# Another order of the work inside a turn of the chunked RWKV-7 scan, with the state update split into a part from keys and a part from betas

## The chip, the cores and the metric

The kernel runs on one core of a Trainium2 chip and computes two whole model blocks. The metric is the device time of one execution in microseconds (us). The change touches only one stage, the RWKV-7 scan of the first block.

## What is computed

The scan carries a 64x64 state S for each of 16 heads over the tokens, once forwards and once backwards (256 context tokens first, then 512 latent ones):

```python
def step(s, inp):
    r_t, w_t, kk_t, a_t, k_t, v_t = inp
    s_kk = jnp.einsum('bhvk,bhk->bhv', s, kk_t)
    s = (s * w_t[:, :, None, :] - s_kk[..., None] * (kk_t * a_t)[:, :, None, :]
         + v_t[..., None] * k_t[:, :, None, :])
    return s, jnp.einsum('bhvk,bhk->bhv', s, r_t)
```

w (decay) and a (rate) come from small LoRA products with a tanh and an exp. The kernel does not go token by token: it takes chunks of 64 tokens, solves a triangular system within the chunk, and moves the state once for each chunk.

## The kernel before

`stage_rwkv_scan` works on 12 tiles of 128 tokens (two chunks each). Tiles 0 to 3 are context, 4 to 11 latent; even tiles go forwards and odd ones backwards, so tile n takes its state from tile n-2. A loop written out by hand on each engine runs over turns n; in turn n three tiles are under way:

- tile n ("now"): the triangular inverse. TensorE makes the products of the scaled betas and keys (`scores`, L808) and transposes both to token order (`turn`, L814). The inverse is then built in six levels. At each level VectorE transposes AT and masks it (`level_mask`, L1097 and L1105), TensorE multiplies (`level_change`, L833), and VectorE adds (`level_update`, L1114). The sixth level has `last_turn` (L823) on TensorE in place of VectorE's transpose.
- tile n+1 ("next"): its features. TensorE `prep_decay` (L843), `prep_rate` (L852) and `prep_sums` (L861); ScalarE `prep_tanh`, `prep_factor` and `prep_exp`; VectorE `prep_decay`, `prep_rates` (L1124, L1125), `prep_kappa`, `prep_beta`, `prep_rr` and `prep_ktil`. The last of these sends `featured`, after which SyncE issues the loads of the tile after it: three of `rkk` (512 KB each), then `hw` and two of `ha` (32 KB each), then V. `prep_decay` on TensorE waits for the last `ha`.
- tile n-1 ("previous"): its two chunk steps. TensorE `b_times_v` (L877), `kappa_times_state` (L886), `inverse_times` (L899) and `to_state` (L913 from the keys, L919 from the betas), with ScalarE copies between them (`take_w` L1042, `take_u` L1048) and VectorE `new_state` (L1152, L1155); for a latent tile `output_from_state` (L933), `output_from_tile` (L945) and `add_output` (L1162).

Each engine takes its own list in order, so an instruction that waits holds up all behind it on that engine. No scheduler decides anything: the order of the work is the order of the calls in the four loops.

Of the kernel before, what the change touches and what calls it, by code (L numbers as in the profile page):

```python
# [659 lines left out]
def stage_rwkv_scan(k, y):  # L660

    nc, t = k.nc, k.t
    HP = D // P
# [4 lines left out]
    C = CHUNK  # L668
    with ExitStack() as s:
# [42 lines left out]
        def need(engine, signal, count):  # L712
            if count > 0:
                engine.wait_ge(signal, count)
# [7 lines left out]
        def steps(n):  # L722
            return 1 if n >= TILES - 2 else 2
# [44 lines left out]
        with nc.Block() as block:  # L768
# [33 lines left out]
            def _(pe):  # L802
# [34 lines left out]
                def prep_decay(n):  # L837
                    need(pe, hid_landed, 48 * (n + 1))
                    if n == 0:
                        pe.wait_ge(weights_in, 128)  # L840
                    need(pe, tok_taken, 2 * n - 1)
                    for j in range(2):
                        mm = pe.matmul(k.ps[:, 4 + j, :], hw[:, :], w2[:, n % 2, j * 512:(j + 1) * 512],  # L843
                                       start=True, stop=True)
                    mm.then_inc(decay_ps, 1)
# [54 lines left out]
                                       wb[r, h * C:(h + 1) * C], start=True, stop=True)  # L900
                    mm.then_inc(u_ps, 1)

                def to_state(n, step):
                    r = rows_of(chunk_of(n, step))
                    if step == 0 and n + 2 < TILES:
                        need(pe, exped, n + 3)
                    elif step == 0:
                        need(pe, tok_taken, 2 * min(n + 2, TILES) - 1)
                        need(pe, state_new, states(n - 1))
                    if step < steps(n):  # L910
                        for h in range(2 * HP):
                            cols = slice(h * C, (h + 1) * C)
                            pe.matmul(k.ps[half(h), 4 + step, hcols(h)], tok_k[r, n % 2, cols], V[r, n % 3, cols],  # L913
                                      start=h < 2, stop=False)
                    need(pe, u_taken, 2 * n + step + 1)
                    if step < steps(n):
                        for h in range(2 * HP):
                            cols = slice(h * C, (h + 1) * C)
                            mm = pe.matmul(k.ps[half(h), 4 + step, hcols(h)], tok_b[r, n % 2, cols], ub[r, cols],  # L919
                                           start=False, stop=h >= 2 * HP - 2)  # L920
                        mm.then_inc(to_ps, 1)
# [28 lines left out]
                for n in range(-1, TILES + 1):  # L950
                    now, nxt, prev = 0 <= n < TILES, n + 1 < TILES, n >= 1
                    if now:
                        need(pe, featured, n + 1)
                        need(pe, w_taken, 2 * n - 1)
                        need(pe, u_taken, 2 * n - 2)
                        scores(beta, kappa[n % 3], 2, n).then_inc(at_ps, 1)
                        need(pe, state_new, states(n - 2))
                        turn(beta, 4)
                        need(pe, y_added, outputs(n - 2))
                        turn(ktil, 6)  # L960
                        need(pe, at_sb, 2 * n + 2)
                        scores(ktil, kappa[n % 3], 2, n).then_inc(bt_ps, 1)
                        level_change(n, 0)
                        if is_lat(n):
                            need(pe, tok_taken, 2 * n + 2)
                            scores(beta, rr[n % 3], 6, n).then_inc(qt_ps, 1)
                    if nxt:
                        prep_decay(n + 1)
                    if now:
                        if is_lat(n):  # L970
                            need(pe, bt_sb, n + 1)
                            scores(ktil, rr[n % 3], 2, n).then_inc(gt_ps, 1)
                    if nxt:
                        prep_rate(n + 1)
                    if now:
                        level_change(n, 1)
                    if prev:
                        inverse_times(n - 1, 0)
                    if nxt:
                        prep_sums(n + 1)  # L980
                    if now:
                        level_change(n, 2)
                    if prev:
                        b_times_v(n - 1, 1)
                    if prev:
                        to_state(n - 1, 0)
                    if now:
                        level_change(n, 3)
                    if prev:
                        kappa_times_state(n - 1, 1)  # L990
                    if prev and is_lat(n - 1):
                        output_from_state(n - 1)
                    if now:
                        level_change(n, 4)
                    if prev:
                        inverse_times(n - 1, 1)
                        to_state(n - 1, 1)
                    if now:
                        last_turn(n)
                        b_times_v(n, 0)  # L1000
                        kappa_times_state(n, 0)
                    if prev and is_lat(n - 1):
                        output_from_tile(n - 1)
                    if now:
                        level_change(n, 5)

            @block.scalar
            def _(act):
# [43 lines left out]
                for n in range(-1, TILES + 1):  # L1052
                    now, nxt, prev = 0 <= n < TILES, n + 1 < TILES, n >= 1
                    if now:
                        take_tokens(n, 0, 4, tok_b[:, n % 2, :])
                        take_tokens(n, 1, 6, tok_k[:, n % 2, :])
                    if nxt:
                        prep_tanh(n + 1)
                    if prev:
                        take_u(n - 1, 0)  # L1060
                    if nxt:
                        prep_factor(n + 1)
                        prep_exp(n + 1)
                    if prev:
                        take_w(n - 1, 1)
                        take_u(n - 1, 1)
                    if now:
                        take_w(n, 0)
# [10 lines left out]
            def _(dve):  # L1079
# [46 lines left out]
                    dve.drain()  # L1126

                def prep_kappa(n):
                    need(dve, exped, n + 1)
                    dve.tensor_tensor(kappa[n % 3][:, :, :], kappa[n % 3][:, :, :], rkk[:, 2, :, :], ALU.mult)  # L1130

                def prep_beta(n):
                    dve.scalar_tensor_tensor(beta[:, :, :], rate[:, :, :], -0.5, ktil[:, :, :], ALU.mult, ALU.mult)

                def prep_rr(n):
                    ends = (63, 127) if n % 2 == 0 else (0, 64)
                    for c in range(2):
                        dve.tensor_copy(pend[:, n % 3, :, c:c + 1], rr[n % 3][:, :, ends[c]:ends[c] + 1])
                    dve.drain()
                    dve.tensor_tensor(rr[n % 3][:, :, :], rr[n % 3][:, :, :], rkk[:, 0, :, :], ALU.mult)  # L1140
# [34 lines left out]
                for n in range(-1, TILES + 1):  # L1175
                    now, nxt, prev = 0 <= n < TILES, n + 1 < TILES, n >= 1
                    if now:
# [1 line left out]
                        level_mask(n, 0)  # L1179
                        need(dve, bt_ps, n + 1)  # L1180
                        kept(BT[:, n % 2, :, :], 2, n, 1, bt_sb)
                        level_update(n, 0)
                        if is_lat(n):
                            need(dve, qt_ps, outputs(n))
                            kept(QT[:, n % 2, :, :], 6, n, 0, qt_sb)
                        level_mask(n, 1)
                        if is_lat(n):
                            need(dve, gt_ps, outputs(n))
# [2 lines left out]
                        prep_decay(n + 1)  # L1191
                    if now:
                        level_update(n, 1)
                    if nxt:
                        prep_rates(n + 1)
                    if now:
                        level_mask(n, 2)
                        level_update(n, 2)
                    if now:
                        level_mask(n, 3)  # L1200
                    if nxt:
                        prep_kappa(n + 1)
                    if prev:
                        new_state(n - 1, 0)
                    if now:
                        level_update(n, 3)
                    if nxt:
                        prep_beta(n + 1)
                    if now:
                        level_mask(n, 4)  # L1210
                        level_update(n, 4)
                    if nxt:
                        prep_rr(n + 1)
                    if now:
                        level_mask(n, 5)
                    if prev:
                        new_state(n - 1, 1)
                    if nxt:
                        prep_ktil(n + 1)
                    if now:  # L1220
                        level_update(n, 5)
                    if prev and is_lat(n - 1):
                        add_output(n - 1)


def load_projection(k, sp, wb, w):
# [2278 lines left out]
```

## Time and profile before

| | us |
|---|---|
| median of 3 runs | 3871.27 (3870.48 to 3876.23) |
| the profiled execution, its own time | 3880.0 |
| its span (first to last instruction) | 3878.2 |
| TensorE matmuls busy in the span | 3172.6 (82%) |
| VectorE busy | 1162.1 (30%) |
| ScalarE busy | 543.6 (14%) |

Shares are of the whole span, of which the scan is about a sixth. A wait in the timeline stands in brackets behind the row that came after it: `[6.77 <-DVE X L1105]` is 6.77 us of idle time of this engine, ended by VectorE's write of X in line 1105. TensorE's times are modelled, and its rows overlap a little; the distance between two starts is the better measure of what a piece takes.

### The profile page before, as it was taken

To read this page: it belongs to the slowest core of one execution; us is meant where nothing else is said; L and a number is where in the kernel's file an instruction comes from. 1 tells how busy PE (TensorE), PEld (TensorE's weight loads), DVE (VectorE), ACT (ScalarE), POOL (GpSimd) and SP (SyncE) were. 2 spreads that over 40 slices of the span, in tenths; PEclk is the share of its full clock that TensorE was granted. 3 is DMA by queue.
4 is the path that set the end of the run, shared out by engine and by line. 5 is a ranking of instruction groups with operands and counts; after the bars stand their busy time and mean duration, and the time that the engine had idled before them with its cause. 6 is when DMAs were issued, how large, how long until landed. Compare 5 with 4: busy or idle time off the path is not lost. (4 is left out here: it accounts for less than half of the span.)

```text
span 3878.2 us, 61816 instructions
## 1 busy us (share of the span) xinstructions
PE 3172.6 (82%) x27303; PEld 2177.5 (56%) x27303; DVE 1162.1 (30%) x1926; ACT 543.6 (14%) x995; POOL 139.7 (4%) x146
## 2 busy tenths in 40 slices
PE   3998577887879899997699999994896587877874
PEld 1453376777753344444599999892344344544442
DVE  0302566666643211245311111103004472101002
ACT  0001223222220100001100001002001141100000
POOL 0000000000010000000100000000000000100000
PEclk8999689889997899997799999996995599899997
DMA  8322311101040622640577777652200103899994
GB/s 351 109 69 69 90 48 48 48 25 48 26 149 0 149 86 70 225 171 13 197 277 249 261 276 239 235 198 69 91 22 1 59 1 138 341 426 427 427 427 157
DMA packets 246708, 612.13 MB, mean 158 GB/s; under 512 B 27188, under 2 KB 136278, under 8 KB 230968
## 3 DMA queue, kind: packets, MB, share of 16 engines
q1 hardware_dynamic: 217704, 522.93, 36.5%
q10 hardware_dynamic: 15968, 54.41, 3.6%
q0 software_dynamic: 12784, 30.99, 2.9%
q8 instruction: 212, 3.47, 0.4%
q14 instruction: 40, 0.33, 0.0%
HBM read 565.64 MB, written 42.63 MB: 157 GB/s over the span
## 5 line engine op out<-in xcount | busy, mean ns | idle before, releaser
L2646 PE MATMUL ps<-moe_xt,moe_wb 128*128 128x152 f32 (+1 forms) x3520 | 457.0, 292 | 2.3 <-DVE moe_xt L2808 2.3
L2646 PEld LDWEIGHTS ps<-moe_xt,moe_wb 128*128 128x128 f32 x3520 | 452.3, 193 | 2.8 <-issue 2.0
L1612 PE MATMUL ps<-ffn_h,ffn_wb 128*128 128x512 f32 x704 | 304.3, 595 | 15.5 <-PEq L1507 15.5
L2326 PE MATMUL ps<-hier_wb,hier_xt 128*64 128x256 f32 x2048 | 244.9, 395 | 72.2 <-DMA hier_wb<-in_expert_w_up 44.0
L833 PE MATMUL ps<-AT,X 64*64 64x64 f32 x4608 | 181.7, 241 | 109.9 <-DVE X L1105 100.5
L2326 PEld LDWEIGHTS ps<-hier_wb,hier_xt 128*64 128x64 f32 x2048 | 161.3, 142 | 167.6 <-issue 62.8
L1612 PEld LDWEIGHTS ps<-ffn_h,ffn_wb 128*128 128x128 f32 x704 | 134.5, 191 | 185.3 <-issue 185.3
L833 PEld LDWEIGHTS ps<-AT,X 64*64 64x64 f32 x4608 | 170.4, 155 | 117.4 <-DVE X L1105 105.3
L2653 PE MATMUL ps<-moe_hT,moe_wb 128*128 128x152 f32 (+1 forms) x1760 | 227.2, 290 | 0.0
L2653 PEld LDWEIGHTS ps<-moe_hT,moe_wb 128*128 128x128 f32 x1760 | 222.7, 190 | 0.0
L1681 PE MATMUL ps<-ffn_g,ffn_wd 128*128 128x512 f32 x352 | 153.0, 598 | 2.6 <-PEq L1575 2.6
L2342 PE MATMUL ps<-hier_wb,hier_actT 128*64 128x512 f32 x512 | 120.3, 612 | 19.8 <-DMA hier_wb<-in_expert_w_down 13.1
L2929 PE MATMUL ps<-in_u,in_wb 128*128 128x512 f32 x256 | 112.8, 603 | 10.0 <-PEq L2856 10.0
L2812 DVE SCALAR_TENSOR_TENSOR moe_th<-moe_th,ps 128x152 f32<-128x152 f32 (+1 forms) x110 | 33.9, 308 | 286.1 <-ACT moe_th L2746 286.1
L1681 PEld LDWEIGHTS ps<-ffn_g,ffn_wd 128*128 128x128 f32 x352 | 67.4, 192 | 88.2 <-issue 88.2
L460 DVE SCALAR_TENSOR_TENSOR mix<-xx,vec,h 128x768 f32<-128x768 f32 (+1 forms) x48 | 43.6, 967 | 185.7 <-PE ps L528 152.7
L1114 DVE TENSOR_TENSOR AT<-AT,ps 128x512 f32<-128x512 f32 x120 | 81.0, 684 | 56.3 <-PE ps L833 55.9
L1640 DVE SCALAR_TENSOR_TENSOR ffn_th<-ffn_th,ps 128x512 f32<-128x512 f32 x22 | 15.1, 686 | 273.2 <-ACT ffn_th L1625 273.2
L2746 ACT ACTIVATE moe_th<-ps 128x152 f32<-128x152 f32 (+1 forms) x110 | 32.3, 294 | 421.0 <-PE ps L2646 421.0
L2929 PEld LDWEIGHTS ps<-in_u,in_wb 128*128 128x128 f32 x256 | 49.5, 194 | 73.1 <-issue 73.1
L2462 DVE COPY hier_xt<-ps 128x1024 f32<-128x1024 f32 x16 | 19.6, 1224 | 219.9 <-PE ps L2318 219.9
L2342 PEld LDWEIGHTS ps<-hier_wb,hier_actT 128*64 128x64 f32 x512 | 36.8, 139 | 80.5 <-issue 63.5
(487 smaller groups left out, 4055.5 us busy)
## 6 DMA issues: line engine op xcount, KB each, us to landing
moe_wb<-in_moe_w SPq DMA_DIRECT2D x60, 2048.0 KB, 10.4
hier_wb<-in_expert_w_gate SPq DMA_DIRECT2D x32, 2048.0 KB, 37.4
hier_wb<-in_expert_w_up SPq DMA_DIRECT2D x32, 2048.0 KB, 37.4
hier_wb<-in_expert_w_down SPq DMA_DIRECT2D x32, 2048.0 KB, 38.6
moe_wb<-in_moe_w SPq DMA_DIRECT2D x30, 1536.0 KB, 7.8
wb_ada<-in_ada_w SPq DMA_DIRECT2D x8, 3072.0 KB, 18.6
ada_late<-in_ada_w ACTq DMA_DIRECT2D x8, 3072.0 KB, 9.6
ffn_wb<-in_ffn_w SPq DMA_DIRECT2D x22, 1024.0 KB, 7.6
```

What stands on the lines that cost most here:

```text
L460: return dve.scalar_tensor_tensor(mix[:, n % 2, c, own], xx[:, c, own], k.v(f"mu{order[n]}")[:, c:c + 1], h[:, c, own], ALU.mult, ALU.add)
L833: mm = pe.matmul(k.ps[rows_of(c), g, q * C:(q + 1) * C], X[rows_of(c), at, :], AT[rows_of(c), at, :], start=True, stop=True)
L1114: dve.tensor_tensor(m, m, bank8(g), ALU.add).then_inc(updated, 1)
L1612: mm = pe.matmul(k.ps[:, bank + q, :], wb[:, j, q, c, o * P:(o + 1) * P], h[:, c, :], start=c == 0, stop=c == KC - 1)
L1681: mm = pe.matmul(k.ps[:, j, :], wd[:, j, c, :], g[:, c, :], start=c == 0, stop=c == FC - 1)
L2326: mm = pe.matmul(k.ps[both_halves(a), bank, 0:256], xs[:, c, :], wb[:, slot, at:at + 256], start=c == 0, stop=c == KC - 1)
L2342: mm = pe.matmul(k.ps[both_halves(a), 7, :], at_sb[:, c, :], wb[:, slot, at:at + 512], start=c == 0, stop=c == 3)
L2646: mm = pe.matmul(k.ps[:, bank, 0:width], wb[:, slot, at:at + P], xs[:, c, :], start=c == 0, stop=c == KC - 1)
L2653: mm = pe.matmul(out_columns(o, width), wb[:, slot, at:at + P], hT[:, f, 0:width], start=f == 0 and o % 3 == 0, stop=f == FC - 1 and (o % ...
L2746: return act.activation(th[:, slot, 0:width], k.ps[:, bank, 0:width], ACT.Tanh, scale=0.5)
L2812: dve.scalar_tensor_tensor(th[:, slot, 0:width], th[:, slot, 0:width], 1.0, k.ps[:, gate, 0:width], ALU.add, ALU.mult)
L2929: mm = pe.matmul(k.ps[:, e % 6, :], own[:, piece] if kind == "fm" else tokens[:, piece], tokens if kind == "fm" else own, start=c == 0, st ...
```

## The change

The calls in the loops of TensorE, ScalarE and VectorE stand in another order, some waits count one signal more or less to match, and `to_state` is two functions: `keys_to_state` (no wait for `u_taken`, called for both chunk steps together) and `betas_to_state`. No work is added or removed. The diff, cut to what the text speaks of:

```diff
@@ the loop on TensorE @@
-                    need(pe, tok_taken, 2 * n - 1)
+                    need(pe, tok_taken, 2 * n)
...
                         scores(beta, kappa[n % 3], 2, n).then_inc(at_ps, 1)
+                        need(pe, y_added, outputs(n - 2))
+                        turn(ktil, 6)
                         need(pe, state_new, states(n - 2))
                         turn(beta, 4)
-                        need(pe, y_added, outputs(n - 2))
-                        turn(ktil, 6)
                         need(pe, at_sb, 2 * n + 2)
                         scores(ktil, kappa[n % 3], 2, n).then_inc(bt_ps, 1)
-                        level_change(n, 0)
                         if is_lat(n):
-                            need(pe, tok_taken, 2 * n + 2)
+                            need(pe, tok_taken, 2 * n + 1)
                             scores(beta, rr[n % 3], 6, n).then_inc(qt_ps, 1)
                     if nxt:
                         prep_decay(n + 1)
                     if now:
+                        level_change(n, 0)
+                    if nxt:
+                        prep_rate(n + 1)
...
                         level_change(n, 1)
-                    if prev:
-                        inverse_times(n - 1, 0)
                     if nxt:
                         prep_sums(n + 1)
+                    if prev:
+                        b_times_v(n - 1, 1)
                     if now:
                         level_change(n, 2)
                     if prev:
-                        b_times_v(n - 1, 1)
-                    if prev:
-                        to_state(n - 1, 0)
+                        inverse_times(n - 1, 0)
+                        keys_to_state(n - 1, 0)
+                        keys_to_state(n - 1, 1)
+                        betas_to_state(n - 1, 0)
...
+                        inverse_times(n - 1, 1)
                     if now:
                         level_change(n, 4)
                     if prev:
-                        inverse_times(n - 1, 1)
-                        to_state(n - 1, 1)
+                        betas_to_state(n - 1, 1)
                     if now:
+                        b_times_v(n, 0)
                         last_turn(n)
-                        b_times_v(n, 0)
@@ the loop on ScalarE @@
                         prep_tanh(n + 1)
-                    if prev:
-                        take_u(n - 1, 0)
-                    if nxt:
                         prep_factor(n + 1)
                         prep_exp(n + 1)
                     if prev:
+                        take_u(n - 1, 0)
                         take_w(n - 1, 1)
@@ the loop on VectorE @@
                         level_update(n, 1)
+                        level_mask(n, 2)
                     if nxt:
                         prep_rates(n + 1)
                     if now:
-                        level_mask(n, 2)
                         level_update(n, 2)
...
+                        level_mask(n, 4)
                     if nxt:
+                        prep_rr(n + 1)
                         prep_beta(n + 1)
...
+                        level_mask(n, 5)
                     if nxt:
-                        prep_rr(n + 1)
+                        prep_kappa(n + 1)
+                        prep_ktil(n + 1)
+                    if prev and is_lat(n - 1):
+                        add_output(n - 1)
                     if now:
-                        level_mask(n, 5)
+                        level_update(n, 5)
                     if prev:
                         new_state(n - 1, 1)
-                    if nxt:
-                        prep_ktil(n + 1)
-                    if now:
-                        level_update(n, 5)
-                    if prev and is_lat(n - 1):
-                        add_output(n - 1)
```

VectorE's list from the second `level_update` (L1114, the second row) to the third, in a latent turn before (`x` is memory that rate, beta, ktil and tmp share):

```order
L1118 TENSOR_SCALAR lw<-lw 128x1024
L1114 TENSOR_TENSOR AT<-AT,ps 128x512 x2
L1124 SCALAR_TENSOR_TENSOR x<-x,rkk 128x1024
L1125 TENSOR_TENSOR x<-x,rkk 128x1024
L1097 STREAM_TRANSPOSE Y<-AT 128x512 x2
L1105 TENSOR_TENSOR X<-Y,sq 128x512 x2
L1114 TENSOR_TENSOR AT<-AT,ps 128x512 x2
```

And the same place in the changed kernel, whose line numbers are three higher here:

```order
L1121 TENSOR_SCALAR lw<-lw 128x1024
L1117 TENSOR_TENSOR AT<-AT,ps 128x512 x2
L1100 STREAM_TRANSPOSE Y<-AT 128x512 x2
L1108 TENSOR_TENSOR X<-Y,sq 128x512 x2
L1127 SCALAR_TENSOR_TENSOR x<-x,rkk 128x1024
L1128 TENSOR_TENSOR x<-x,rkk 128x1024
L1117 TENSOR_TENSOR AT<-AT,ps 128x512 x2
```

The transpose and mask of level 2 now stand ahead of `prep_rates`, which reads what ScalarE's `prep_factor` wrote.

TensorE's list at the start of a latent turn before, from the transposes (L814) to the second level (the second L833):

```order
L814 MATMUL ps<-sq,x 128x128 x16
L808 MATMUL ps<-kappa,x 64x64 x32
L833 MATMUL ps<-AT,X 64x64 x32
L808 MATMUL ps<-rr,x 64x64 x32
L843 MATMUL ps<-w,hw 128x512 x2
L808 MATMUL ps<-rr,x 64x64 x32
L852 MATMUL ps<-ha,a 128x128 x8
L833 MATMUL ps<-AT,X 64x64 x32
```

And in the changed kernel:

```order
L814 MATMUL ps<-sq,x 128x128 x16
L808 MATMUL ps<-kappa,x 64x64 x32
L808 MATMUL ps<-rr,x 64x64 x32
L843 MATMUL ps<-w,hw 128x512 x2
L833 MATMUL ps<-AT,X 64x64 x32
L852 MATMUL ps<-ha,a 128x128 x8
L808 MATMUL ps<-rr,x 64x64 x32
L833 MATMUL ps<-AT,X 64x64 x32
```

The first level (L833) now stands behind `prep_decay` (L843), which waits for the load of `ha`.

## Rows read from the trace of the kernel before

**Rows 1.** Timeline of VectorE: first step of turns 0, 1, 4, 10, 11; last `add_output`.

```profile
448.88 1.29 DVE L1083 TENSOR_TENSOR AT<-ps,sq 128x512 f32<-128x512 f32 x2 [2.13 <-PE ps L808]
...
494.30 1.29 DVE L1083 TENSOR_TENSOR AT<-ps,sq 128x512 f32<-128x512 f32 x2 [0.28 <-PE ps L808]
...
652.36 1.29 DVE L1083 TENSOR_TENSOR AT<-ps,sq 128x512 f32<-128x512 f32 x2 [0.25 <-PE ps L808]
...
992.67 1.28 DVE L1083 TENSOR_TENSOR AT<-ps,sq 128x512 f32<-128x512 f32 x2
...
1051.80 1.28 DVE L1083 TENSOR_TENSOR AT<-ps,sq 128x512 f32<-128x512 f32 x2
...
1111.05 1.22 DVE L1162 TENSOR_TENSOR y<-y,ps 128x1024 f32<-128x1024 f32 x1 [9.95 <-PE ps L945]
```

**Rows 2.** Waits in the scan: engine, line <- releaser: us in total, times, longest.

```profile
PE ps L833 <- DVE X L1105: 100.5, 30, 6.8
...
PE ps L843 <- DMA ha<-hid_d: 5.1, 4, 3.0
```

**Rows 3.** Timeline of TensorE, turn 10.

```profile
1000.65 1.98 PE L843 MATMUL ps<-w,hw 128*128 128x512 f32 x4
...
1017.46 3.68 PE L833 MATMUL ps<-AT,X 64*64 64x64 f32 x64 [6.77 <-DVE X L1105]
1020.93 3.30 PE L877 MATMUL ps<-V,BT 64*64 64x64 f32 x29
...
1027.35 2.95 PE L833 MATMUL ps<-AT,X 64*64 64x64 f32 x58
...
1034.18 2.08 PE L833 MATMUL ps<-AT,X 64*64 64x64 f32 x64 [1.08 <-DVE X L1105]
1036.09 1.97 PE L899 MATMUL ps<-wb,TT 64*64 64x64 f32 x31
...
1040.20 2.03 PE L823 MATMUL ps<-sq,AT 64*64 64x64 f32 x63
1042.07 2.03 PE L877 MATMUL ps<-V,BT 64*64 64x64 f32 x32
1044.16 1.09 PE L886 MATMUL ps<-N,kappa 64*64 64x64 f32 x30
```

**Rows 4.** Timeline of ScalarE, turn 10.

```profile
1008.73 1.02 ACT L1048 ACTIVATE ub<-ps 64x1024 f32<-64x1024 f32 x1 [1.69 <-PE ps L899]
1009.78 3.18 ACT L1026 ACTIVATE x<-x,kar,kah 128x128 f32<-128x128 f32 x8
```

**Rows 5.** Timeline of VectorE, turn 10.

```profile
1006.15 1.42 DVE L1114 TENSOR_TENSOR AT<-AT,ps 128x512 f32<-128x512 f32 x2
1013.09 1.23 DVE L1124 SCALAR_TENSOR_TENSOR x<-x,rkk 128x1024 f32<-128x1024 f32 x1 [5.52 <-ACTq L1028]
...
1016.75 1.25 DVE L1105 TENSOR_TENSOR X<-Y,sq 128x512 f32<-128x512 f32 x2
...
1041.36 0.69 DVE L1105 TENSOR_TENSOR X<-ps,sq 128x512 f32<-128x512 f32 x1 [2.91 <-PE ps L823]
```

**Rows 6.** Stretch 1020 to 1040: PE, PEld, DVE, ACT, POOL busy, granted clock, DMA.

```profile
1020.00:1040.00 20.00, 18.74 (x432) 18.47 (x430) 13.42 (x21) 2.04 (x2) 1.80 (x2) 0.76 0.01 3
```

**Rows 7.** Timeline of SyncE's queue ahead of turn 2.

```profile
543.30 0.55 SPq L775 DMA_DIRECT2D rkk<-r_d  x1
```

**Rows 8.** Timeline of TensorE, turn 2.

```profile
554.11 2.69 PE L843 MATMUL ps<-w,hw 128*128 128x512 f32 x4 [2.98 <-DMA ha<-hid_d]
556.74 2.07 PE L852 MATMUL ps<-ha,a 64*128 64x128 f32 x16
...
584.92 2.84 PE L833 MATMUL ps<-AT,X 64*64 64x64 f32 x64 [2.88 <-DVE X L1105]
```

**Rows 9.** Timeline of TensorE, start of turn 10.

```profile
995.22 0.33 PE L814 MATMUL ps<-sq,x 128*128 128x128 f32 x1 [1.43 <-issue]
...
999.52 0.27 PE L833 MATMUL ps<-AT,X 64*64 64x64 f32 x1 [1.03 <-issue]
```

More of the change, by code:

```diff
@@ L901, in inverse_times, with keys_to_state, betas_to_state @@
                     mm.then_inc(u_ps, 1)
-                def to_state(n, step):
+                def keys_to_state(n, step):
+                    if step == steps(n):
+                        return
                     r = rows_of(chunk_of(n, step))
-                    if step == 0 and n + 2 < TILES:
+                    if n + 2 < TILES:
                         need(pe, exped, n + 3)
-                    elif step == 0:
-                        need(pe, tok_taken, 2 * min(n + 2, TILES) - 1)
+                    else:
+                        need(pe, tok_taken, 2 * min(n + 2, TILES))
                         need(pe, state_new, states(n - 1))
[L910 to L914, printed above, removed]
+                    for h in range(2 * HP):
+                        cols = slice(h * C, (h + 1) * C)
+                        pe.matmul(k.ps[half(h), 4 + step, hcols(h)], tok_k[r, n % 2, cols], V[r, n % 3, cols],
+                                  start=h < 2, stop=False)
+                def betas_to_state(n, step):
+                    r = rows_of(chunk_of(n, step))
                     need(pe, u_taken, 2 * n + step + 1)
@@ L969, in _ @@
                     if now:
+                        level_change(n, 0)
+                    if nxt:
+                        prep_rate(n + 1)
+                    if now:
                         if is_lat(n):
@@ L972, in _ @@
                             scores(ktil, rr[n % 3], 2, n).then_inc(gt_ps, 1)
-                    if nxt:
-                        prep_rate(n + 1)
-                    if now:
                         level_change(n, 1)
-                    if prev:
-                        inverse_times(n - 1, 0)
                     if nxt:
                         prep_sums(n + 1)
+                    if prev:
+                        b_times_v(n - 1, 1)
                     if now:
@@ L990, in _ @@
                         kappa_times_state(n - 1, 1)
-                    if prev and is_lat(n - 1):
-                        output_from_state(n - 1)
+                        if is_lat(n - 1):
+                            output_from_state(n - 1)
+                        inverse_times(n - 1, 1)
                     if now:
@@ L1054, in _ @@
                     if now:
-                        take_tokens(n, 0, 4, tok_b[:, n % 2, :])
-                        take_tokens(n, 1, 6, tok_k[:, n % 2, :])
+                        take_tokens(n, 0, 6, tok_k[:, n % 2, :])
+                        take_tokens(n, 1, 4, tok_b[:, n % 2, :])
                     if nxt:
                         prep_tanh(n + 1)
-                    if prev:
-                        take_u(n - 1, 0)
-                    if nxt:
                         prep_factor(n + 1)
@@ L1128, in prep_kappa @@
                 def prep_kappa(n):
-                    need(dve, exped, n + 1)
                     dve.tensor_tensor(kappa[n % 3][:, :, :], kappa[n % 3][:, :, :], rkk[:, 2, :, :], ALU.mult)
@@ L1135, in prep_rr @@
                 def prep_rr(n):
+                    need(dve, exped, n + 1)
                     ends = (63, 127) if n % 2 == 0 else (0, 64)
@@ L1181, in _ @@
                         kept(BT[:, n % 2, :, :], 2, n, 1, bt_sb)
-                        level_update(n, 0)
                         if is_lat(n):
@@ L1185, in _ @@
                             kept(QT[:, n % 2, :, :], 6, n, 0, qt_sb)
+                        level_update(n, 0)
                         level_mask(n, 1)
@@ L1196, in _ @@
                     if now:
-                        level_mask(n, 2)
                         level_update(n, 2)
-                    if now:
                         level_mask(n, 3)
-                    if nxt:
-                        prep_kappa(n + 1)
                     if prev:
@@ L1206, in _ @@
                         level_update(n, 3)
+                        level_mask(n, 4)
                     if nxt:
+                        prep_rr(n + 1)
                         prep_beta(n + 1)
                     if now:
-                        level_mask(n, 4)
                         level_update(n, 4)
+                        level_mask(n, 5)
                     if nxt:
-                        prep_rr(n + 1)
+                        prep_kappa(n + 1)
+                        prep_ktil(n + 1)
+                    if prev and is_lat(n - 1):
+                        add_output(n - 1)
                     if now:
-                        level_mask(n, 5)
+                        level_update(n, 5)
                     if prev:
                         new_state(n - 1, 1)
-                    if nxt:
-                        prep_ktil(n + 1)
-                    if now:
-                        level_update(n, 5)
-                    if prev and is_lat(n - 1):
-                        add_output(n - 1)
 def load_projection(k, sp, wb, w):
```

## The prediction

> **What bounds the kernel now.** I read the timeline of VectorE first, since its first step of a turn stands once in each turn: the scan's turns begin at 448.88 and end with the last add at 1111.05, which ends about 1112.3 [rows 1]. So turns 0 to 3 take 652.36 - 448.88 = 203.5 us, turns 4 to 10 take 1051.80 - 652.36 = 399.4 us (57.1 each), and turn 11 with the tail takes 60.5. Outside the scan nothing changes.
>
> Next the waits of the scan: TensorE waited 100.5 us for X, 30 times, by far its largest wait [rows 2]. The timeline of TensorE in turn 10 shows where: it sits idle 6.77 us before level 2 (start 1017.46) [rows 3]. VectorE's timeline says why. It had finished level 1's update at 1006.15 + 1.42 = 1007.57, but its next instruction in order is `prep_rates`, which started only at 1013.09, after 5.52 us idle, behind ScalarE; level 2's mask comes behind that, at 1016.75 [rows 5]. ScalarE took `ub` at 1008.73, which waited for TensorE, and only then ran the eight `prep_factor` steps, 3.18 us [rows 4]. So the chain that sets the turn there is TensorE's `inverse_times`, ScalarE's copy, `prep_factor`, `prep_rates`, the mask, TensorE. Level 2 itself needs none of it.
>
> The idle time has a second price. After it level 2 took 3.68 us where level 4 took 2.08 [rows 3], and the mean granted clock of 1020 to 1040 is 0.76 [rows 6]: TensorE had fallen to the lower of its two levels (1.2 of 2.4 GHz). In turn 10, start to start: level 2 took 1020.93 - 1017.46 = 3.47 against 1036.09 - 1034.18 = 1.91 (1.56 lost), `b_times_v` 3.30 against 2.03 (1.27), level 3 2.95 against 2.08 (0.87), and the 6.42 between them holds about 1 us more for the two products into the state, by the same ratio. That is 4.7 us.
>
> **The change part by part.** No instruction is added or removed, so all of it is waits. A turn can't be shorter than TensorE's own work in it. At the higher clock, from the distances of starts: a level 1.91 (six of them, 11.5), `inverse_times` and `last_turn` about 1.9 each (5.7 for three), `b_times_v` 2.09 twice (4.2), `kappa_times_state` about 0.98 twice (2.0) [rows 3]; the other pieces I take in proportion to their matmuls (scores 1.09 four times, transposes 2.05, `prep_decay` 1.92, `prep_rate` 1.09, sums 2.0, keys and betas 0.97 four times, output 3.9). Together about 42.7.
>
> (1) *Level 2's mask ahead of `prep_rates`, and `take_u` behind `prep_exp`.* VectorE runs the mask straight behind level 1's update; `prep_factor` no longer waits for `inverse_times`. TensorE has `prep_sums` (2.0) and `b_times_v` (2.1) to do while VectorE masks (2.4), so level 2 finds its X. This removes 6.8 and, since TensorE then doesn't fall to the lower clock, up to 4.7.
>
> (2) *`inverse_times(n-1, 1)` ahead of level 4, masks 4 and 5 and the features in the gaps.* The later waits of 1.08 for X go [rows 3], with about 0.2 for `ub`. Chunk 1 of the state is then formed by `new_state` as the last step of VectorE's turn; the first reader, the transposes of beta, is put second for this, and by hand comes out 0.2 late. VectorE's steps stand between a mask and its update, where they hide behind the product; it is busy for about 36 us of the turn, less than TensorE.
>
> (3) *`prep_decay` ahead of level 0.* This adds a wait. `featured` comes after mask 5 now: mask 5 starts about 1.2 after `last_turn` starts (1041.36 against 1040.20 [rows 3, 5]), takes 1.6, and kappa and ktil 2.3, so `featured` is 5.1 after `last_turn`. TensorE ends its turn 6.7 after `last_turn` (1.9, 1.0, 1.9 and level 5 1.9). The load of `ha` ahead of turn 2 was started after its `featured` at 543.3 and TensorE went on at 554.11 [rows 7, 8]: 10.8 us. That wait is the longest of four [rows 2], so the other loads came sooner; I take 10, between 9.5 and 10.8. So `ha` lands some 8.5 us (8.0 to 9.2) into the new turn, and TensorE is there after 5.7. It would wait 2.8, with level 0 and all else queued behind. But TensorE also has gaps that nothing explains but issue, of 1.43 and 1.03 in turn 10, just while these loads run [rows 9], about 3.2 us a turn. They fall into the same stretch, so wait and gaps together cost about 3.6, only 0.4 more than the gaps alone. What VectorE does then is behind level 0, so nothing else hides this wait.
>
> (4) *Keys and betas split.* TensorE's keys of both steps fill the time of ScalarE's copy `ub`; this closes the waits of 0.2 and costs nothing. Its cover is `prep_exp`, which must be over: by hand it ends 1 to 3 us before the keys.
>
> For turn 10: 59.1 - 6.8 - 1.2 - 4.7 = 46.4, plus what is new: 0.4 at `ha`, 0.4 at the start (beta and AT), 0.5 before level 1 where VectorE's mask ends a little late: 47.7. Summing the pieces in the new order gives the same from the other side: 42.7 + 3.6 + 0.4 + 0.5 = 47.2. I take 47.4.
>
> Turns 4 to 10: 7 x 47.4 = 331.8, of which turn 4 is about 2 shorter (no output yet) and turn 5 about 2 longer (its `ha` comes later): 399.4 - 331.8 = 67.6 saved.
>
> Turns 0 to 3 have no output and fewer scores, so TensorE reaches `prep_decay` after 4.9, while `featured` comes only 0.2 after the turn's start: `ha` at about 10.4, a wait of 5.5. By hand turn 0 goes from 45.4 (494.30 - 448.88) to about 40, since it waits for `ha` as it does now and loses the wait before level 2. Turns 1 to 3, 52.7 each now, lose the 6.7 before level 2, 2.9 before level 4 [rows 8] and some 3 of low clock, and take on 4.1 more of waiting for `ha` (5.5 against 1.4 on average), 2 at a lower clock after it, and 1 at `take_w`: 47.2; I take 48. Saved: 203.5 - 184 = 19.5.
>
> Turn 11 and the tail: no `ha` to wait for, chain of levels as now; `b_times_v` in the tail no longer stands behind the last level. About 4.5.
>
> Sum: 67.6 + 19.5 + 4.5 = 91.6. A schedule leaves out small misses, so I take off 1 us in each of turns 0 to 10: 81 saved. Against the profiled execution's own 3880.0 that is 3799; the median of the runs is 8.7 below that execution, so 3871.3 - 81 = 3790.
>
> **A rule that speaks against the change.** After the 2.98 us wait for `ha` in turn 2, `prep_decay` took 2.69 (1.98 in turn 10) and `prep_rate` 2.07, about twice the 1.09 used above [rows 3, 8]: 1.6 us lost behind one wait. The Trainium skill, "TensorE: Matmul & The Clock Gate", Part 1, says that the default state is throttled and activity releases it, so every idle stretch invites the lower clock; the trace agrees. By that rule the new wait for `ha` would be followed by the lower clock in each turn, and the sum would be that of the first rival.
>
> **The rivals.** *First: the wait for `ha` cools TensorE in every turn.* For it: 2.98 us was enough in turn 2, and the new wait is about 2.8 in latent turns and 5.5 in context turns. Against it: in latent turns it is broken up by gaps of issue, after which the clock stayed up in turn 10. Price: between 1.6 (as in turn 2) and 4.7 (as after 6.77) for 11 turns, at 3.5 some 38, of which the 1 us a turn taken off above covers 8 at least: 81 - 30 = 51 saved, about 3820.
>
> *Second: the stall only moves.* `inverse_times`, `ub` and the betas now stand behind `prep_sums` and `prep_exp`, and VectorE's `new_state(n-1, 0)` waits for them ahead of level 3's update. If that chain comes as late as `prep_rates` did, TensorE is idle 6.8 before level 4 instead of level 2, and nothing is won: 3865 to 3877. Against it: by hand the copy ends while the keys still run.
>
> *Third: slower.* Only the load of `ha` could do this, being in front of the whole inverse. It pays for the change if it costs 7.4 us a turn more than taken (81 / 11), that is if it lands about 17.5 us after `featured` instead of 10. Then each further us costs 11: at 20 us the time is 3871 + 27 = 3898. The wait seen, 10.8 at its longest, says no; what could is that `featured` itself comes late, behind `prep_kappa` and `prep_ktil`.
>
> *Fourth: better than taken.* No small misses, gaps and wait fully on top of each other, no low clock: the 91.6 and up to 10 more: 3770 to 3778.
>
> **How the numbers follow.** The forecast 0.65, with a range of its own of 3778 to 3808; the first rival 0.17; the second 0.05; the third 0.04; the fourth 0.09. To leave out no more than 2 in 10 the range takes the forecast, most of the fourth and of the first: 3768 to 3830. A change of 0.2% (7.7 us) is about what a measurement of this kernel can tell from none. Faster by more: 0.90; within it: 0.05; slower: 0.05.
>
> **What would show it.** Right: latent turns of 47 to 49 us between VectorE's L1083 steps (now L1086), no idle time of TensorE before level 2, granted clock near 1 through a latent turn, waits of TensorE at `prep_decay` of 1 to 3 us in latent and about 5 in context turns. Wrong: a wait above 3 us at L833, at the betas or at `kappa_times_state`; a `prep_decay` of over 2.5 us in latent turns (first rival); VectorE idle before `new_state(n-1, 0)` for several us (second).

## The result and the profile after

The changed kernel takes 3781.57 us (median of 4 runs, 3773.33 to 3786.8) against 3873.75 before (4 runs): 92.2 us less, a ratio of 0.976 (95% interval 0.974 to 0.9781). The forecast was 3790. The two profiled executions stand at 3880.0 and 3782.05, 98 us apart; the rows and turn times of this section compare these two.

VectorE's first step of a turn (now L1086), in the timeline of the changed kernel, answers [rows 1]; these are turns 0, 1, 4, 8, 9 and 11, then the last `add_output`:

```profile
448.70 1.29 DVE L1086 TENSOR_TENSOR AT<-ps,sq 128x512 f32<-128x512 f32 x2 [2.14 <-PE ps L808]
...
496.00 1.28 DVE L1086 TENSOR_TENSOR AT<-ps,sq 128x512 f32<-128x512 f32 x2
...
635.28 1.28 DVE L1086 TENSOR_TENSOR AT<-ps,sq 128x512 f32<-128x512 f32 x2
...
820.73 1.28 DVE L1086 TENSOR_TENSOR AT<-ps,sq 128x512 f32<-128x512 f32 x2
...
866.17 1.28 DVE L1086 TENSOR_TENSOR AT<-ps,sq 128x512 f32<-128x512 f32 x2
...
956.64 1.28 DVE L1086 TENSOR_TENSOR AT<-ps,sq 128x512 f32<-128x512 f32 x2
...
1012.48 1.22 DVE L1165 TENSOR_TENSOR y<-y,ps 128x1024 f32<-128x1024 f32 x1 [9.89 <-PE ps L949]
```

| us | before | forecast | after |
|---|---|---|---|
| turns 0 to 3 | 203.5 | 184 | 186.6 |
| turns 4 to 10 | 399.4 | 331.8 | 321.4 |
| turn 11 and tail | 60.5 | 56 | 57.1 |

So the scan is 98.4 us shorter, and that is all of the difference between the two profiled executions. The waits of the scan (TensorE's, as [rows 2]) show what was traded:

```profile
PE ps L843 <- DMA ha<-hid_d: 27.3, 10, 5.4
PE ps L833 <- DVE X L1108: 18.2, 16, 3.9
```

The wait for X fell from 100.5 to 18.2, and the wait for `ha` rose from 5.1 to 27.3. In latent turn 8 TensorE hardly stops (timeline, against [rows 3]); `...` marks rows left out:

```profile
826.26 1.98 PE L843 MATMUL ps<-w,hw 128*128 128x512 f32 x4 [0.55 <-DMA ha<-hid_d]
828.17 2.08 PE L833 MATMUL ps<-AT,X 64*64 64x64 f32 x64
...
837.22 2.02 PE L877 MATMUL ps<-V,BT 64*64 64x64 f32 x31
839.13 1.97 PE L833 MATMUL ps<-AT,X 64*64 64x64 f32 x62
...
856.42 1.97 PE L823 MATMUL ps<-sq,AT 64*64 64x64 f32 x62
```

Level 2 (839.13) follows `b_times_v` with no wait where it waited 6.77, and each piece is at the higher clock. The window view of the next turn, turn 9 (866 to 911), has a granted clock of 1.00, with TensorE busy for 41.82 of 45 us (the columns are those of [rows 6]):

```profile
866.00:911.00 45.00, 41.82 (x1287) 39.04 (x1286) 37.81 (x58) 15.80 (x30) 2.50 (x2) 1.00 0.20 52
```

Turn 1 shows the other side, against [rows 8]:

```profile
504.25 3.78 PE L843 MATMUL ps<-w,hw 128*128 128x512 f32 x4 [5.41 <-DMA ha<-hid_d]
507.96 2.11 PE L833 MATMUL ps<-AT,X 64*64 64x64 f32 x64
```

TensorE waits 5.41 us for `ha`, and `prep_decay` then takes 3.78, the lower clock, against 1.98 in turn 8. Of the 27.3 us, 25.2 lie in turns 0 to 5 (3.4 to 5.4 each), where `prep_decay` takes 3.3 to 3.8 each time; in turns 6 to 9 the waits are 0.4 to 0.7 and it takes 1.98. Turn 0 got longer, 47.3 us against 45.4 (494.30 - 448.88). TensorE's timeline of turn 0:

```profile
456.37 3.33 PE L843 MATMUL ps<-w,hw 128*128 128x512 f32 x4 [4.06 <-DMA ha<-hid_d]
459.63 2.36 PE L833 MATMUL ps<-AT,X 64*64 64x64 f32 x64
...
469.23 2.08 PE L833 MATMUL ps<-AT,X 64*64 64x64 f32 x64 [0.59 <-DVE X L1108]
475.25 3.68 PE L833 MATMUL ps<-AT,X 64*64 64x64 f32 x64 [3.94 <-DVE X L1108]
481.50 3.68 PE L833 MATMUL ps<-AT,X 64*64 64x64 f32 x64 [2.58 <-DVE X L1108]
```

The same turn in the kernel before:

```profile
453.54 2.04 PE L833 MATMUL ps<-AT,X 64*64 64x64 f32 x64
456.39 1.98 PE L843 MATMUL ps<-w,hw 128*128 128x512 f32 x4 [0.81 <-DMA ha<-hid_d]
...
469.46 3.68 PE L833 MATMUL ps<-AT,X 64*64 64x64 f32 x64 [5.56 <-DVE X L1105]
```

`prep_decay` starts at the same time in both, behind `ha`. The first level started before it at 453.54 and now starts behind it at 459.63, 6.1 us later. The wait before level 2 shrank by 5.0 (5.56 to 0.59), which doesn't make that up. There is no previous tile to fill the waits before levels 3 and 4, which run at the lower clock.

### The profile page after: what moved, and what is told of

Read it like the earlier page. It is cut to its first block and busy times, and to the rows that moved or that the text cites. A ratio compares the mean times of both kernels' runs of the same rounds, so it can differ in the third digit from the quotient of the medians.

```text
span 3780.2 us, 61815 instructions
## 1 busy us (share of the span) xinstructions
PE 3135.7 (83%) x27303; PEld 2137.2 (57%) x27303; DVE 1156.4 (31%) x1926; ACT 544.7 (14%) x995; POOL 138.8 (4%) x146
## 5 line engine op out<-in xcount | busy, mean ns | idle before, releaser
L1611 PE MATMUL ps<-ffn_h,ffn_wb 128*128 128x512 f32 x704 | 304.3, 595 | 15.5 <-PEq L1506 15.5
L833 PE MATMUL ps<-AT,X 64*64 64x64 f32 x4608 | 162.5, 224 | 21.3 <-DVE X L1108 18.2
L833 PEld LDWEIGHTS ps<-AT,X 64*64 64x64 f32 x4608 | 152.1, 139 | 37.0 <-DVE X L1108 20.7
## 6 DMA issues: line engine op xcount, KB each, us to landing
hier_wb<-in_expert_w_down SPq DMA_DIRECT2D x32, 2048.0 KB, 38.6
```

What stands on the lines that cost most here:

```text
L833: mm = pe.matmul(k.ps[rows_of(c), g, q * C:(q + 1) * C], X[rows_of(c), at, :], AT[rows_of(c), at, :], start=True, stop=True)
L1611: mm = pe.matmul(k.ps[:, bank + q, :], wb[:, j, q, c, o * P:(o + 1) * P], h[:, c, :], start=c == 0, stop=c == KC - 1)
```

## The experiments

Twelve kernels, each against runs of the kernel before on the same chip. A last column gives the distance to the changed kernel's own gain of 92.2. Each interval reaches 5 to 12 us to either side, so a distance of less than some 14 us in that column tells nothing by itself.

| kernel | gain on before, us | ratio (95%) | against the change |
|---|---|---|---|
| e1: before, mask 2 earlier | 56.7 | 0.984 (0.9814 to 0.9866) | -35.5 |
| e2: before, `take_u` later | 29.7 | 0.9914 (0.989 to 0.9938) | -62.5 |
| e3: before, both | 88.7 | 0.9763 (0.9734 to 0.9792) | -3.5 |
| e10: before, both, `ha` first | 97.3 | 0.9746 (0.9721 to 0.977) | +5.1 |
| e6: before, `ha` first | 4.4 | 0.9989 (0.9975 to 1.0003) | -87.8 |
| e11: change, mask 2 undone | 50.9 | 0.9868 (0.9842 to 0.9894) | -41.3 |
| e12: change, `take_u` undone | -10.1 | 1.0032 (1.0019 to 1.0046) | -102.3 |
| e8: change, `inverse_times` undone | 51.3 | 0.9868 (0.9839 to 0.9897) | -40.9 |
| e7: change, keys undone | 85.3 | 0.9779 (0.9749 to 0.9809) | -6.9 |
| e4: change, level 0 ahead of `prep_decay` | 120.2 | 0.968 (0.9659 to 0.9701) | +28.0 |
| e5: change, `ha` first | 130.8 | 0.9663 (0.9639 to 0.9687) | +38.6 |
| e9: change, e4 and e5 | 131.8 | 0.9656 (0.9632 to 0.968) | +39.6 |

**e1, mask 2 alone, on the kernel before.**

```diff
                         level_update(n, 1)
+                    if now:
+                        level_mask(n, 2)
                     if nxt:
                         prep_rates(n + 1)
                     if now:
-                        level_mask(n, 2)
                         level_update(n, 2)
```

> The kernel before, with one edit: on VectorE the mask of level 2 stands ahead of prep_rates. Theory 1 (most of the gain is the broken chain ScalarE's factor, prep_rates, mask 2, level 2): the wait of 6.8 us before level 2 and the low clock behind it go, prep_rates still starts where it did, so level 2's update comes about 5 us earlier and level 3's about 8: 55 to 90 us faster. Theory 2 (the gain is in the many small fillings of the new order, the keys and betas, inverse_times ahead of level 4): under 30 us faster, with the idle time moved to level 3.

56.7 us faster, the low end of theory 1. The timeline of TensorE in turn 8 of e1 shows what is left:

```profile
859.18 2.08 PE L833 MATMUL ps<-AT,X 64*64 64x64 f32 x64
861.10 2.03 PE L877 MATMUL ps<-V,BT 64*64 64x64 f32 x32
864.76 1.39 PE L913 MATMUL ps<-V,tok_k 64*64 64x64 f32 x32 [1.63 <-ACTq L1037]
...
867.61 3.34 PE L833 MATMUL ps<-AT,X 64*64 64x64 f32 x58
```

Level 2 has no wait, but the keys now wait for `prep_exp`, which still stands behind `take_u`, and level 3 is at the lower clock.

**e2, `take_u` alone, and e3, both, on the kernel before.**

```diff
-                    if prev:
-                        take_u(n - 1, 0)
                     if nxt:
                         prep_factor(n + 1)
                         prep_exp(n + 1)
                     if prev:
+                        take_u(n - 1, 0)
                         take_w(n - 1, 1)
```

> The kernel before, with one edit: on ScalarE take_u(n-1, 0) stands behind prep_factor and prep_exp. Theory 1: prep_rates comes 2.8 us earlier, mask 2 still behind it, so TensorE still waits about 4 us before level 2 and still falls to the low clock: 25 to 50 us faster. Theory 2: nothing to speak of, under 10 us.

> The kernel before with both edits, mask 2 ahead of prep_rates and take_u behind prep_exp, and TensorE's list untouched. Theory 1: all that the change brings, 80 to 110 us faster, since level 0 still stands ahead of prep_decay and no new wait for ha arises; it could be faster than the full change. Theory 2: 30 to 50 us, the rest needs TensorE's new order.

29.7 and 88.7 us, both inside theory 1's ranges: two moved calls, with TensorE's list untouched, give nearly what the whole change gives. The intervals of e3 and of the change overlap. On the kernel before the two parts add up: 56.7 + 29.7 = 86.4.

**e11 and e12, the same two undone in the changed kernel.**

> The changed kernel with one part undone: prep_rates stands ahead of mask 2 on VectorE again. prep_factor now ends near where level 1's update does, so only prep_rates' own 2.3 us come ahead of the mask, and TensorE has the sums and b_times_v to do: it waits about 2 us before level 2. 20 to 40 us slower than the changed kernel (3802 to 3822). If the mask's place were what all of the gain hangs on, 55 us or more.

> The changed kernel with one part undone: take_u(n-1, 0) stands ahead of prep_factor on ScalarE again. Since TensorE's inverse_times(n-1, 0) now stands behind level 2, factor, prep_rates and level 2's update would all wait for it, some 8 us a turn and the low clock behind it: 80 to 120 us slower than the changed kernel, so nothing of the gain is left. Rival: ScalarE has 5 us to spare before the sums, and it costs under 30 us.

e11 loses 41.3, just above the 20 to 40 expected. TensorE waits before level 2 as foreseen, in its turn 8:

```profile
873.99 2.08 PE L833 MATMUL ps<-AT,X 64*64 64x64 f32 x64 [2.06 <-DVE X L1108]
```

e12 loses 102.3, as expected, and is 10.1 us slower than the kernel before. VectorE's `prep_rates` and TensorE's keys in its turn 8, from two timelines:

```profile
920.35 1.22 DVE L1129 SCALAR_TENSOR_TENSOR x<-x,rkk 128x1024 f32<-128x1024 f32 x1 [8.59 <-ACTq L1033]
```

```profile
923.45 3.00 PE L914 MATMUL ps<-V,tok_k 64*64 64x64 f32 x58 [7.49 <-ACTq L1042]
```

With `inverse_times` behind level 2, `take_u` ahead of `prep_factor` holds up the features, level 2's update behind them and the keys at once. In the forecast such a move of the stall was the second rival; with this one call in its old place it comes about.

**e8, `inverse_times(n-1, 1)` behind level 4 again.**

```diff
-                        inverse_times(n - 1, 1)
                     if now:
                         level_change(n, 4)
                     if prev:
+                        inverse_times(n - 1, 1)
                         betas_to_state(n - 1, 1)
```

> The changed kernel with one part undone: inverse_times(n-1, 1) stands behind level 4 again. By my sum it fills the 1.1 us (latent) to 2.9 us (context) that TensorE waits for mask 4: 10 to 20 us slower than the changed kernel. Rival: the wait only moves to the copy wb or ub, since inverse_times waits 1.1 us for wb in context turns now: within 5 us of the changed kernel.

40.9 us slower than the change: both expectations were wrong. In turn 8 level 4 doesn't wait in e8; the wait is at the betas, for the copy `ub`:

```profile
875.68 2.08 PE L833 MATMUL ps<-AT,X 64*64 64x64 f32 x64
877.60 2.03 PE L899 MATMUL ps<-wb,TT 64*64 64x64 f32 x32
880.73 1.15 PE L923 MATMUL ps<-ub,tok_b 64*64 64x64 f32 x32 [1.11 <-ACT ub L1053]
881.72 2.37 PE L877 MATMUL ps<-V,BT 64*64 64x64 f32 x31
...
883.94 3.16 PE L823 MATMUL ps<-sq,AT 64*64 64x64 f32 x62
```

1.11 us of waiting, and then 0.4 in `b_times_v` and 1.2 in `last_turn` (3.16 against 1.97) at the lower clock: 2.7 of the 3.5 us that this turn is longer (895.02 - 846.13 = 48.9 against 45.4). The same 1.11 stands at the betas in each of turns 1 to 10; in turns 1 to 4 level 4 also waits 1.7 for its mask. So in most turns `inverse_times` ahead of level 4 pays by hiding ScalarE's copy `ub` behind the level, not by filling the wait for the mask.

The kernel before had the same two pieces behind level 4 and waited only 0.17 there. Its turn 10:

```profile
1036.09 1.97 PE L899 MATMUL ps<-wb,TT 64*64 64x64 f32 x31
1037.95 1.10 PE L913 MATMUL ps<-V,tok_k 64*64 64x64 f32 x31
1039.23 1.08 PE L919 MATMUL ps<-ub,tok_b 64*64 64x64 f32 x29 [0.17 <-ACT ub L1048]
```

There the keys (L913) of that step stood between `inverse_times` and the betas and covered the copy. The split took them away, so e8 has no cover left, and by these rows its 40.9 is the price of the two orders together and not the worth of `inverse_times` ahead of level 4 in the kernel before. e8 with the keys beside the betas again was not run.

**e7, the keys of step 1 beside its betas again.**

> The changed kernel with one part undone: the keys of chunk step 1 stand just ahead of its betas again, not beside those of step 0. By my sum the split costs and brings nothing: within 5 us of the changed kernel. Rival: the keys of both steps together cover ScalarE's copy of ub, and without them TensorE waits 1 us at the betas of step 0 in each turn: 8 to 12 us slower than the changed kernel.

6.9 us slower than the change by the medians, with intervals that overlap by more than that, and its waits for `ub` sum to 2.1 us (12 times, at most 0.2) against 0.4. The rival's 1 us a turn isn't there (with `inverse_times` ahead of level 4 the copy is covered in either case); whether the split brings a few us stays open.

**e4, level 0 ahead of `prep_decay` again; e5 and e6, the loads of `hw` and `ha` first; e9, e4 and e5 together; e10, e3 and `ha` first.** The edit of e5 in SyncE's `load_tile`:

```diff
-                    need(sp, featured, n)
-                    for m, src in enumerate((k.r_d, k.k_d, k.kk_d)):
-                        sp.dma_start(rkk[:, m, :, :], src[:, :, at0:at0 + P]).then_inc(rkk_landed, 16)
                     need(sp, rate_ps, n)
...
                         sp.dma_start(ha[rows_of(e), :], k.hid_d[1, lora, at0:at0 + P]).then_inc(hid_landed, 16)
+                    need(sp, featured, n)
+                    for m, src in enumerate((k.r_d, k.k_d, k.kk_d)):
+                        sp.dma_start(rkk[:, m, :, :], src[:, :, at0:at0 + P]).then_inc(rkk_landed, 16)
```

> The changed kernel with one part undone: on TensorE level 0 stands ahead of prep_decay again. If the wait for ha in front of level 0 costs what its rows say (about 4.4 us and the low clock behind it in turns 0 to 3, 3.4 in turns 4 and 5, 0.5 in the later ones), level 0 fills 1.9 us of it and the clock recovers sooner: 8 to 20 us faster than the changed kernel (3762 to 3774). If the wait is hidden anyway by VectorE's chain, no difference (within 4 us of 3781.6).

> The changed kernel with the loads of hw and ha issued on SyncE ahead of the wait for featured and of the three loads of rkk; their buffers are free from prep_rate on. Theory A (prep_decay's wait for ha and the low clock behind it cost turns 0 to 5 some 3 to 7 us each): no wait at prep_decay, prep_decay 1.98 us in context turns, 20 to 40 us faster than the changed kernel (3742 to 3762). Theory B (VectorE's chain of levels bounds the context turns, so the wait is slack): under 8 us.

> The kernel before with the same move of the loads of hw and ha. There prep_decay waited 5.1 us in all, in turns 0 to 3, behind level 0: at most 5 to 10 us faster by either theory. It tells what the move is worth without the changed order.

> Both additions to the changed kernel: the loads of hw and ha first, and level 0 ahead of prep_decay. With no wait for ha left, TensorE still waited 1.49 us before level 1 in context turns, since level 0 stood behind prep_decay; that wait should shrink to 0.5: 3 to 8 us faster than with the loads first alone (3738 to 3744). If VectorE's chain bounds these turns anyway, the same 3746.

> The kernel before with mask 2 ahead of prep_rates, take_u behind prep_exp and the loads of hw and ha first, TensorE's list untouched. These two orders alone gave 88.7 us; the waits for ha left in it are 6.2 us and the low clock behind them: 5 to 15 us faster, 95 to 104 us against before. TensorE's new order should still be worth some 25 us beside it (waits of 1.1 us each before kappa_times_state and level 4 in a latent turn).

e5 is 38.6 us faster than the change, theory A. In its turn 1 (TensorE's timeline, against the 5.41 above):

```profile
495.05 1.96 PE L843 MATMUL ps<-w,hw 128*128 128x512 f32 x4 [0.16 <-ACT tok_b L1016]
496.93 2.08 PE L833 MATMUL ps<-AT,X 64*64 64x64 f32 x64
...
501.59 2.08 PE L833 MATMUL ps<-AT,X 64*64 64x64 f32 x64 [1.49 <-DVE X L1108]
```

The wait is gone and `prep_decay` takes 1.96. Its turns 0 to 3 sum to 612.70 - 452.89 = 159.8 us, against 186.6 with the change, 27 us less; turns 4 to 10 take 925.64 - 612.70 = 312.9 against 321.4. These 35 us are about the waits that went, 27.3, and the 9.9 that six runs of `prep_decay` took beyond 1.98 each. But the move also costs something ahead of turn 0. In e5 VectorE's first step of turn 0, and TensorE's `prep_decay` in it, stand at

```profile
452.89 1.29 DVE L1086 TENSOR_TENSOR AT<-ps,sq 128x512 f32<-128x512 f32 x2 [2.14 <-PE ps L808]
```

```profile
456.55 1.95 PE L843 MATMUL ps<-w,hw 128*128 128x512 f32 x4 [0.16 <-ACT tok_b L1016]
```

against 448.70 and 456.37 in the changed kernel: turn 0 starts 4.2 us later and its `prep_decay` no sooner. All four kernels with these loads first start turn 0 at 451.0 to 452.9, all others at 446.5 to 449.4. Whether the old order for the first tile alone would win this back was not tried.

e4 is 28.0 faster than the change, more than its expectation: level 0 fills the wait, and in turn 1 the wait left is 3.58:

```profile
495.07 2.08 PE L833 MATMUL ps<-AT,X 64*64 64x64 f32 x64 [0.27 <-DVE X L1107]
500.74 3.45 PE L843 MATMUL ps<-w,hw 128*128 128x512 f32 x4 [3.58 <-DMA ha<-hid_d]
```

e9 can't be told from e5, so once `ha` is there in time the place of `prep_decay` makes no difference that these runs show; the 3 to 8 us expected didn't come. e6 shows that the same move is worth nothing that can be told on the kernel before (interval to 1.0003): there level 0 stood ahead of the wait, which was 5.1 us in all, and turn 0 starts 4.0 later (452.90 against 448.88). e10, as expected at 97.3, falls 33.5 us short of e5. The two kernels differ in all the rest of the change: TensorE's order, the split of `to_state`, VectorE's later steps and the order of ScalarE's token copies. With `ha` in time all of this together is worth about that, and no run takes it apart further. Part of it is seen in the waits: e10's TensorE waits 29.0 us for X and 12.7 before `kappa_times_state` (1.1 in each of turns 1 to 10), e5's 15.5 and 1.7.

## Why the prediction was right, and where not

- *The chain before level 2 bounds the scan*: right, shown by e1, e2 and e3 from one side and e11 and e12 from the other. On the kernel before its two parts add up (86.4 of 88.7). In the changed kernel they don't: undoing one costs 41.3 and the other 102.3, together more than the whole gain.
- *The lower clock as a second price, 4.7 us in turn 10*: the turn 8 rows above have it gone, and turn 9 ran at 1.00.
- *Latent turns 47.4*: they took 45.9 on average (321.4 / 7), and turns 6 to 10, of 44.6 to 45.8, came out below the 47 to 49 given as the sign of being right. One step that was too high is the wait for `ha` together with the gaps of issue, taken at 3.6 us; in turn 8 they are 0.55 at `prep_decay` and 1.95 of gaps (1.23 and 0.72). The other is TensorE's own work, taken at 42.7; it was busy for 41.8 in turn 9. The gap of 1.23 falls ahead of `prep_decay` and uses up part of the wait, as supposed. Turns 4 and 5 had next to no such gap and waited 3.4 each, above the 1 to 3 of the forecast.
- *Turn 0 down to 40*: wrong, 47.3. The step put it that the turn waits for `ha` "as it does now" (0.81), but before, level 0 stood ahead of that wait; now it stands behind 4.06 us of it and starts 6.1 us later. The 39.2 of e5 (492.05 - 452.89) doesn't confirm the rest of the step, since that turn starts 4.2 later there and ends only 4.0 sooner than in the changed kernel. Turns 1 to 3, taken at 48, took 46.4 on average.
- *Turn 11 and the tail, 56*: 57.1.
- *1 us a turn taken off for small misses, 11 in all*: this was the largest error. The sum was 91.6, and with the allowance 81; no such misses show. That 91.6 stands so near the 92.2 between the medians is in part luck: the sum was made from rows of the profiled executions, which are 98 us apart. Against these it is 10.4 short in turns 4 to 10, 2.6 too high in turns 0 to 3 and 1.1 too high in turn 11.
- *`inverse_times` ahead of level 4*: named as a gain of 1.08 and 0.2 a turn. In the changed kernel undoing it costs 40.9 (e8), by another mechanism: the split of the keys had taken away what covered the copy `ub`. The forecast, and the 10 to 20 us expected of e8, left this out.
- *Keys and betas split, no cost and the 0.2 at the betas closed*: the waits for `ub` at the betas are 0.4 in all, and e7 can't be told from the change.
- *The first rival*, TensorE cooled by the wait for `ha` in every turn: it came true in six turns of eleven, turns 0 to 5. By the Trainium skill, "TensorE: Matmul & The Clock Gate", Part 1, activity releases the throttle; there the trace agrees (3.78 for `prep_decay` after 5.41 idle, then 2.11 for level 0). In turns 6 to 9, with waits of at most 0.67 there, the lower clock doesn't show.
- *The second rival*, the stall only moves: it didn't come. TensorE has no wait before level 4 in turns 1 to 10, where 6.8 was named; turn 0 alone has 3.94 before level 3.
- *The third rival*, slower by late loads: the loads came as before (in turn 8 `rkk` was issued at 816.63 and `prep_decay` started at 826.26, 9.6 us, against 10 taken); having them in front of the inverse cost about the 38.6 us of e5, not 92.

## What to carry over

Before giving an engine that works in order a new list, find the instruction that waits for another engine ahead of work that doesn't need it; moving two such calls gave 88.7 us here, where the whole change gave 92.2. Then look at what the new list puts in front of the work: a 32 KB load that had been covered stood ahead of the whole inverse, and issuing it ahead of the three 512 KB loads was worth another 38.6. And when a piece is moved, ask what it had been covering: the keys, moved away, left ScalarE's copy bare as soon as `inverse_times` stood behind level 4 (40.9 us). Orders on several engines belong together: the old place of `take_u` costs 102.3 us with TensorE's new list (e12), and 32.0 with the old one (88.7 of e3 less 56.7 of e1).

## What the runs showed of the hardware

A wait of 1.11 us was followed by the lower clock in each of turns 1 to 10 of e8: the main part of `last_turn` takes 2.6 to 3.6 us there, against 1.85 to 1.97 in the changed kernel. In turns 1 to 4 of the changed kernel a wait of the same length left TensorE at the higher one, as here in turn 1:

```profile
528.66 1.90 PE L899 MATMUL ps<-wb,TT 64*64 64x64 f32 x29 [1.11 <-ACT wb L1047]
...
530.57 1.85 PE L833 MATMUL ps<-AT,X 64*64 64x64 f32 x58
```

In e8 `inverse_times` (2.0 us) stood just ahead of the wait; what tells the two cases apart was not tried.

TensorE also has gaps with no wait behind them that the profile shows ("issue"). In turns 6 to 10 of the changed kernel one of 0.8 to 1.7 us stands at `scores` (L808), in the stretch in which the next loads run, and turns 0 to 3 have none. These turns have the same loads, but TensorE waits for `ha` in that stretch, which may cover the gaps. What makes them stays open: the kernel before has two of 0.8 in turn 11, where no `rkk` is loaded any more.
